# The beginning of a two-layer step: token norm from token rows, modulation pairs and projection units interleaved

## The reference, cut to what matters

```python
m = silu(cvec) @ w_ada[l] + b_ada[l]            # (6 * 1024); sh1, sc1, g1, sh2, sc2, g2
h = (x * rsqrt(mean(x * x) + 1e-6) * norm1_g[l]) * (1 + sc1) + sh1
p = h @ w_in[l]                                 # (1024, 2816): q_A, k_A, v_A, u_B, q_C, k_C, v_C
```

## Time and profile before

| | before |
|---|---|
| three runs, us | 1532.72, 1535.53, 1537.12 |
| profiled execution, span from first to last instruction, us | 1532.4 |
| TensorE busy, share of the span | 97% |
| VectorE busy | 61% |
| ScalarE busy | 51% |
| mean granted TensorE clock | 0.991 |
| DMA, mean over the span | 223 GB/s |

### The profile page before, as it was taken

The page is one execution under the profiler, slowest core; times in us unless marked ns, Lnnn a source line. Parts: engine busy times, 40 slices in busy tenths (PEclk is TensorE's granted clock), DMA queues, the critical chain, the costliest instruction groups (busy, mean ns, idle before and its releaser), DMA issues.

```text
span 1532.4 us, 22129 instructions
## 1 busy us (share of the span) xinstructions
PE 1484.4 (97%) x8652; PEld 1306.1 (85%) x8652; DVE 937.5 (61%) x1076; ACT 786.3 (51%) x892; POOL 53.6 (4%) x54
## 2 busy tenths in 40 slices
PE   5999999999999999999999999998999999999997
PEld 4788969689999999998889697898888888888875
DVE  3542265455654354436523665556898898988988
ACT  5434354353532242225333454535778778787875
POOL 0100000000000000001000000000000000000002
PEclk8999999999999999999999999999999999999999
DMA  9754375583763445245333554535899999999994
GB/s 332 242 178 155 110 226 187 178 262 110 231 195 111 125 115 160 84 150 170 121 117 110 180 186 158 193 114 176 313 375 387 379 376 371 380 386 374 377 378 164
DMA packets 236028, 342.36 MB, mean 223 GB/s; under 512 B 8629, under 2 KB 156766, under 8 KB 235694
## 3 DMA queue, kind: packets, MB, share of 16 engines
q1 hardware_dynamic: 227392, 313.32, 60.0%
q0 software_dynamic: 6496, 24.69, 4.4%
q10 hardware_dynamic: 2062, 3.24, 0.6%
HBM read 325.74 MB, written 15.47 MB: 223 GB/s over the span
## 4 chain that ended last, share of the span: by engine, by line
PE 87%; DVE 5%; DMA 3%; ACT 2%; SPq 1%; issue 1%; DVEq 0%; ACTq 0%
PE ps L648 25%; PE ps L650 25%; PE ps L649 25%; PE ps L665 2%; DMA raw<-in_w_ada_dram 2%; DVE wlo L2075 2%; PE ps L831 1%; SPq L446 1%; ACT whi L1508 1%; PE ps L865 1%; PE ps L849 1%; DMA early<-in_w_ada_dram 1%; PE ps L1063 1%; PE ps L731 1%; PE ps L810 0%
## 5 line engine op out<-in xcount | busy, mean ns | idle before, releaser
L648 PE MATMUL ps<-hhi,whi 128*128 128x384 f32 x824 | 276.7, 336 | 0.2
L650 PE MATMUL ps<-hhi,wlo 128*128 128x384 f32 x824 | 275.4, 334 | 0.0
L649 PE MATMUL ps<-hlo,whi 128*128 128x384 f32 x824 | 275.3, 334 | 0.0
L1696 DVE TENSOR_TENSOR wlo<-raw,whi 128x2048 fp32r<-128x2048 f32 x66 | 151.0, 2289 | 179.2 <-ACT whi L1258 165.9
L2075 DVE TENSOR_TENSOR wlo<-raw,whi 128x2048 fp32r<-128x2048 f32 (+1 forms) x81 | 179.0, 2227 | 27.4 <-ACT whi L1508 26.9
L1508 ACT ACTIVATE whi<-raw 128x2048 fp32r<-128x2048 f32 (+1 forms) x81 | 150.5, 1868 | 49.4 <-PE ps L650 49.2
L2075 DVE TENSOR_TENSOR wlo<-mraw,whi 128x2048 fp32r<-128x2048 f32 (+2 forms) x81 | 160.7, 1992 | 16.7 <-ACT whi L1508 16.2
L648 PE MATMUL ps<-whi,xgh 128*128 128x512 f32 (+1 forms) x432 | 163.9, 379 | 4.9 <-DVE wlo L2075 3.7
L1508 ACT ACTIVATE whi<-mraw 128x2048 fp32r<-128x2048 f32 (+2 forms) x81 | 136.6, 1687 | 51.4 <-PE ps L650 51.2
L650 PE MATMUL ps<-whi,xgl 128*128 128x512 f32 (+1 forms) x432 | 161.0, 373 | 0.0
L649 PE MATMUL ps<-wlo,xgh 128*128 128x512 f32 (+1 forms) x432 | 160.8, 372 | 0.0
(11 more groups left out here) (343 smaller groups left out, 2496.1 us busy)
## 6 DMA issues: line engine op xcount, KB each, us to landing
raw<-in_w_ada_dram SPq DMA_DIRECT2D x82, 512.0 KB, 5.6
raw<-in_w_ex_up_dram SPq DMA_DIRECT2D x27, 1024.0 KB, 6.4
raw<-in_w_ex_down_dram SPq DMA_DIRECT2D x27, 1024.0 KB, 5.0
raw<-in_w_gate_dram SPq DMA_DIRECT2D x48, 512.0 KB, 4.7
raw<-in_w_in_dram SPq DMA_DIRECT2D x44, 512.0 KB, 5.7
raw<-in_w_ex_gate_dram SPq DMA_DIRECT2D x18, 1024.0 KB, 7.1
mraw<-in_w_ex_gate_dram SPq DMA_DIRECT2D x18, 1024.0 KB, 7.8
mraw<-in_w_ex_down_dram SPq DMA_DIRECT2D x18, 1024.0 KB, 8.5
```

The lines of the kernel that those rows point to most:

```text
L648: pe.matmul(out, s[0], m[0], start=first, stop=False, **kw)
L649: pe.matmul(out, s[0], m[1], start=False, stop=False, **kw)
L650: return pe.matmul(out, s[1], m[0], start=False, stop=last, **kw)
L1696: dve.tensor_tensor(wlo[:, n % RING, :], raw[:, n % RING, :], whi[:, n % RING, :].bitcast(F32), ALU.subtract).then_inc(lo_done, 1)
```

## The change

Order of loads: only the identity part of the constants (64 KB) comes first, the rest after the modulation slots; the tokens come in three transfers with a semaphore each. Slots are renumbered (`FIRST_ADA`, `FIRST_WIN`): modulation 0 and 1, projection slot 0, modulation 2 and 3, projection slot 2 (the first half of K_A), modulation 4 to 7, projection slots 1 and 3. `win_turn` maps the k-th projection slot in this order. The small loads needed first go first, and lambda and sink have their own semaphore.

Norm: ScalarE squares the token rows as loaded and sums along them in the same instruction (`token_squares`), instead of squares of `xT`, VectorE sums and thin matmuls. VectorE, not ScalarE, copies the turned tokens to `xT`. TensorE spreads the root (`spread`) before modulation pair 0.

Projection: `first_units` does Q_A and the first slot of K_A pair by pair, with the modulation products between. 20 matmuls on the identity, into a bank that is overwritten later, stand before it.

```diff
+FIRST_ADA = (0, 1, 2, 3, 4, 5, 7, 9)
+FIRST_WIN = {0: 6, 2: 8, 1: 10, 3: 12}
+EARLY_BUF = {0: 0, 1: 1, 2: 2, 3: 3, 4: 4, 5: 0, 7: 1, 9: 2}
 # SyncE
+            sp.dma_start(ident, const[:, 0:P]).then_inc(const_in, 16)
+            for b in range(BLK):
+                sp.dma_start(xtok[:, b, :], a["x_sample"][0, (b - 1) * P:b * P] if b else a["x_prompt"][0]).then_inc(x_in[b], 16)
+            modulation(0, range(0, 2))
             projection_slot(0, 0)
+            modulation(0, range(2, 4))
+            projection_slot(0, 2)
+            modulation(0, range(4, 8))
+            sp.dma_start(cst[:, P:C_POOL], const[:, P:C_POOL]).then_inc(const_in, 16)
             projection_slot(0, 1)
...
 # TensorE
+            def first_units(products):
+                def pair(u, p, b):
+                    return products(u, b, (2 * p, 2 * p + 1))
+                pe.wait_ge(x_ev, BLK)
+                pe.wait_ge(lo_done, split_count(win_slot(0, 0) + 1))
+                pe.wait_ge(h_ready, 1)
+                for b in range(BLK):
+                    if b == 2:
+                        ada_pair(1)
+                    pair(Q_A, 0, b)
+                ada_end(0, 1)
+                pe.wait_ge(lo_done, split_count(win_slot(0, 2) + 1))
+                for b in range(BLK):
+                    if b == 2:
+                        ada_pair(2)
+                    pair(K_A, 0, b)
+                ada_end(0, 2)
+                pe.wait_ge(h_ready, 2)
+                for b in range(BLK):
+                    mm = pair(Q_A, 1, b)
+                mm.then_inc(mm_done, 1)
+                pe.wait_ge(ada_read, 3)
+                for b in range(BLK):
+                    if b == 2:
+                        ada_product(0, 6)
+                    mm = pair(K_A, 1, b)
+                mm.then_inc(mm_done, 1)
+                ada_product(0, 7)
+                ada_end(0, 3)
+                pe.wait_ge(lo_done, split_count(win_slot(0, 1) + 1))
+                for p in (2, 3):
+                    pe.wait_ge(h_ready, p + 1)
+                    for b in range(BLK):
+                        mm = pair(Q_A, p, b)
...
+                ada_product(1, 0)
...
             pe.wait_ge(const_in, 16)
             for b in range(BLK):
+                pe.wait_ge(x_in[b], 16)
                 for k in range(KD):
                     mm = pe.transpose(...)
                 mm.then_inc(x_tr, 1)
+                if b == 0:
+                    pe.wait_ge(init_in, 16 * n_init)
...
+            pe.wait_ge(v_ev, 2)
+            spread(0)
             pe.wait_ge(silc_ready, 1)
             pe.wait_ge(pick_ready, 1)
             ada_pair(0)
             ada_end(0, 0)
             pe.wait_ge(x_ev, BLK)
-            ada_pair(1)
-            ada_end(0, 1)
-            pe.wait_ge(ones_set, 1)
-            mean_squares(0)
-            ada_pair(2)
-            ada_end(0, 2)
+            for n in range(20):
+                pe.matmul(ps[:, 5, 0:P], ident, ident, start=True, stop=True)
 # ScalarE
             def ada_group(g):
+                act.wait_ge(mm_done, ada_slot(0, 2 * g + 1) + 1)
+                act.activation(adarow[:, :], ps[:, 7, 0:256], copy).then_inc(ada_row, 1)
+                if g == 0:
+                    hi(win_turn(0, 0))
                 act.wait_ge(ada_turned, g + 1)
...
+            def token_squares(b):
+                act.wait_ge(x_in[b], 16)
+                act.activation(xsq[:, b, :], xtok[:, b, :], ACT.Square, accum_out=rcol[:, 1, b:b + 1]).then_inc(sq_done, 1)
...
 # ScalarE, modulate(0): before pair p of the channel tiles
                         if p == 1:
+                            hi(win_turn(0, 1))
                         if p == 3:
+                            hi(win_turn(0, 2))
                             act.activation(lamp[:, :, :], lamp[:, :, :], ACT.Exp).then_inc(v_ev, 1)
+                        if p:
+                            ada_group(p)
 # VectorE
             def first_norm():
                 reciprocal_root(0)
+                for p in range(4):
                     scaled(0, p)
+                link(dve.tensor_tensor(lamprod[:, :, :], lamrow[:, :, 0, :], lamrow[:, :, 1, :], ALU.mult))
+                dve.tensor_reduce(lamp[:, :, :].rearrange("p l i -> p (l i)"), lamprod[:, :, :], X, ALU.add).then_inc(lam_sums, 1)
+                for p in range(4):
+                    first_modulations(p)
                     dve.wait_ge(mods_ready, p + 1)
                     shifted(0, p)
+                    if p < 3:
+                        lo(win_turn(0, p))
+                    h_low(0, p)
```

More of the change, by code:

```diff
@@ L700, in mean_squares @@
                     residual_turned(0)
[L701 to L705, removed]
+                spread(i)
                 if i in (1, 2):
@@ L732, in rot_transposes @@
                 mm.then_inc(tr_done, 1)
+            def first_units(products):
[30 more added lines that the diff above has]
+                    pe.wait_ge(h_ready, p + 1)
+                    for b in range(BLK):
+                        mm = pair(Q_A, p, b)
+                        if p == 3 and b < 2:
+                            mm.then_inc(proj_block, 1)
+                mm.then_inc(mm_done, 1)
+                ada_product(1, 0)
             def input_projection(l):
@@ L753, in input_projection @@
                         pe.matmul(proj_out(Q_A)[:, b, :], hlo[:, 0, b * P:(b + 1) * P], w[0], start=False, stop=False)
-                for p in range(4):
+                for p in range(4 if l else 0):
                     pe.wait_ge(h_ready, 8 * l + p + 1)
@@ L758, in input_projection @@
                     for b in range(BLK):
-                        if l == 0 and p == 1 and b == 2:
-                            ada_pair(3)
-                        mm = products(Q_A, b, (2 * p, 2 * p + 1) if p or l == 0 else (1,))
+                        mm = products(Q_A, b, (2 * p, 2 * p + 1) if p else (1,))
                         if p == 3 and b < 2:
@@ L779, in input_projection @@
                                 mm.then_inc(proj_block, 1)
-                            if i == 0 and b and u <= V_A:
+                            if i == (l == 0 and u == K_A) and b and u <= V_A:
                                 ti = 2 * (u - 1) + b - 1
@@ L1590, in _ @@
                            ACT.Silu).then_inc(silc_ready, 1)
-            for b in range(BLK):
-                act.wait_ge(x_tr, b + 1)
-                act.activation(xT[:, :, b * P:(b + 1) * P],
-                               ps[:, 2 * b:2 * b + 2, :].rearrange("p a (k t) -> p (a k) t", t=P), copy).then_inc(x_ev, 1)
-            act.wait_ge(x_ev, BLK)
-            for m0, m1 in ((0, 2), (2, 4), (4, 6), (6, 7), (7, 8)):
-                square(m0, m1)
-            ada_group(0)
-            act.wait_ge(ones_set, 1)
-            table(ACT.Sqrt)
-            ada_group(1)
-            hi(win_slot(0, 0))
-            root(0)
+            token_squares(1)
+            token_squares(2)
+            table(ACT.Sqrt)
+            root(0)
+            ada_group(0)
             act.wait_ge(lam_sums, 1)
@@ L1615, in _ @@
                             turned_evac(l, ti)
-                    if l == 0 and len(slots) == 2:
-                        hi(win_slot(l, slots[0] + 2))
+                    if l == 0 and len(slots) == 2 and u != K_A:
+                        hi(win_turn(l, slots[0] + 2 + (u == Q_A)))
                     if l == 0 and u == U_B:
@@ L1624, in _ @@
                     if l == 0:
-                        hi(win_slot(l, slots[-1] + 2))
+                        hi(win_turn(l, slots[-1] + 2 + (u == Q_A)))
                 pool_copy(l)
@@ L2210, in _ @@
                 for u, slots in enumerate(PROJ_SLOTS):
-                    if l or len(slots) == 2:
-                        lo(win_slot(l, slots[0] + 2))
+                    if l or (len(slots) == 2 and u != K_A):
+                        lo(win_turn(l, slots[0] + 2 + (l == 0 and u == Q_A)))
                     if l and len(slots) == 2:
                         lo(win_slot(l, slots[1] + 2))
+                    if l == u == 0:
+                        dve.wait_ge(const_in, 32)
                     if u < N_ROT:
@@ L2217, in _ @@
                     if l == 0:
-                        lo(win_slot(l, slots[-1] + 2))
+                        lo(win_turn(l, slots[-1] + 2 + (u == Q_A)))
                 for o in range(3):
```

116 lines of the change are left out of this document (50 added, 66 removed).

## The result

| | before | changed |
|---|---|---|
| runs, us (median; lowest to highest) | 1534.46 (1532.72 to 1537.12), 4 runs | 1545.67 (1541.93 to 1546.68), 4 runs |
| ratio to before, 95% interval | | 1.0065, 1.0051 to 1.0079 |
| profiled execution, span, us | 1532.4 | 1539.8 (its run: 1541.93, the lowest of the four) |

The change costs 0.65%, about 10 us, where 0.6 us of gain was forecast. (A ratio here is not the quotient of the two medians: those are 11.2 us apart.) The first part of the page of the changed kernel, to be read against the earlier trace rows: 22 matmuls and 22 weight loads more.

What follows compares the result with a forecast made beforehand. TensorE's late first projection product (34.83 us, behind the sixth modulation slot) and the low clock were taken to bound the beginning. 2.5 us gained minus 1.9 for one low spell gave 0.6: 1534.9 us, range 1530.0 to 1538.5.

Steps and rivals of the forecast that it cites:

- The ledger of the beginning: Step-by-step times from inputs to the mark: 64.6 against 67.05, 2.5 us gained if the clock stays up.
- Spread done: Norm on ScalarE, then TensorE's spread at the low clock level, 1.65 us, finished at 15.8 us; before, 29.2.
- pair 1: First modulation pair, queued behind the spread: 32 matmuls at the low clock level, 3.9 us, done at 19.7.
- first product: TensorE's first product of the input projection, forecast at 26.6 us, 8.2 us earlier than 34.83.
- gap: TensorE idle 3.6 us before K_A, waiting for VectorE's low half behind the second modulation; K_A starts at 36.6.
- one low spell: One low-clock stretch, after the dummies or behind the gap, taken as 1.9 us lost; chance 0.42.
- the mark: 67.05 us before: Q_A, K_A's first half, two transpose groups and the next modulation phase's first product done; forecast 64.6.
- The rival with the clock as the bound: Dummies don't lift the clock and it is low again after the gap: 3.1 us lost, 1538.6; chance 0.18.
- The price of the dummies: 20 dummy matmuls before the projection, 4.3 us at 0.216 each, from 21.2 to 25.5, said to cost nothing.
- The step that failed: Behind the mark both kernels have the same work and order, so the change is worth the mark's shift, 2.5 us.
- but for the transposes: Exception to same work behind the mark: one group of transposes before it, the other group counted as 0.6 us.
- The prediction's own sign of this: Stretches behind the mark differing by more than a microsecond would show the change acts somewhere not counted.

Runs made afterwards that it cites:

- 9 dummies: Changed kernel with 9 identity matmuls of 128 columns in place of 20; 1539.71 us, ratio 1.0033.
- 9 wide: Changed kernel with 9 dummy matmuls of 288 columns in place of 20 of 128; 1537.02 us, ratio 1.0014.
- 9 wide with both mends: Changed kernel with 9 dummies of 288 columns, K_A's low half before the second modulation, Q_A's transposes together behind K_A's second slot's block 1; 1529.31 us, ratio 0.9964.
- 9 thin with both: 9 wide with both mends, but its 9 dummies have one column each; median 1531.72 us, ratio 0.9981.
- before with 11: Kernel before plus 11 dummy matmuls where TensorE waits 2.69 us for the first row copy; 1541.57 us, ratio 1.0043.
- transposes together: Changed kernel with both groups of Q_A's transposes behind block 1 of K_A's second slot; 1542.35 us, one run.
- low half first: Changed kernel with VectorE's low half of K_A's first slot ahead of the second modulation; 1537.50 us, one run.
- 31 dummies: Changed kernel with 31 dummy matmuls in place of 20; 1539.03 us, ratio 1.0025.
- 31 with both mends: Changed kernel with 31 dummies, K_A's low half first and both transposes behind block 1 of K_A's second slot; 1533.18 us, ratio 0.999.
- before with 22: Kernel before plus 22 dummy matmuls at the same place as in before with 11; 1538.02 us, ratio 1.0018.

## Why the prediction was wrong

All kernels, sorted by the matmul and load records that TensorE has over the 2 x 8652 of the kernel before, all of them ahead of the loop. The last column says how the distance to the kernel before changes between 500 and 562 us, over the turn of the loop (the same matmuls laid beside each other; positive is lost):

| added | kernels | the branch, us | idle at the pass's first matmul | stall at its 15th | pieces fetched in the second pass | over the turn, us |
|---|---|---|---|---|---|---|
| 0 | before, 9 dummies, 9 wide, 9 wide with both mends, 9 thin with both | 4.0 to 4.4 | 1.2 to 1.6 | none | 9 | -0.3 to 0.1 |
| 44 | changed (twice), before with 11, transposes together, low half first | 3.3 to 3.9 | 0.5 to 1.1 | 2.1 to 2.9 | 9 | 3.0 to 4.1 |
| 88 | 31 dummies, 31 with both mends, before with 22 | 0.23 to 0.24 | none | none | 0 | -1.8 |

Point by point:

- **The ledger of the beginning** held. Spread done at 14.9 (forecast 15.8), pair 1 at 18.3 (19.7), first product 24.96 (26.6), gap 3.57 (3.6) with VectorE's low half ending it, K_A 35.30 (36.6), one low spell of 3.4 us right behind the gap and none at the first products, 1.1 us won at the mark (0.6). The landings and the order on VectorE were read well enough. The rival with the clock as the bound had the right side, a loss, by luck: of its two low spells only the one behind the gap is there, the beginning was a gain all the same, and the loss came from elsewhere and is larger than its 3.1 us. The price of the dummies was luck too: 20 transposes at the low level, 0.216 us each, where they are 40 records at the high level, 0.12 each. And the spread ran at the high level (0.91 us, forecast 1.65), while the low spell came behind it, from 15.0 to 18.4.
- **The step that failed** stands in "What bounds the kernel now": "From the mark on both kernels have the same work in the same order, but for the transposes, so the change is worth what it moves the mark by." Same work and same order are not the same program. TensorE's stream got 44 instructions longer ahead of the dense loop. That costs 0.43%, 6.6 us, by two pairs of kernels: 11 dummies in the kernel before (1.0043), and nine wide dummies for twenty narrow ones in the changed one (1.0057 to 1.0014; by the ends of the two intervals 0.13% to 0.74%). I priced the dummies by their time, 4.3 us beside VectorE's chain; that time was near (4.71 us, and nothing waited for them) and beside the point. The prediction's own sign of this came out: "if the stretches behind the mark differ by more than a microsecond, the change acts somewhere that I didn't count".
- **A smaller miss in the same sentence**: "but for the transposes". The second group stands right ahead of Q_C and adds a wait of 1.0 us to the 0.6 that it costs as work anywhere, and that eats what the mark had won. Together with the gap it was worth mending: from nine wide dummies to the same with both mends, 1.0014 to 0.9964, 0.5%.
- **The sum, as measured** in the later runs: 0.57% = 0.43% for the place of the instructions + 0.14% that are left with nine wide dummies, which the gap, its low spell and the transposes more than cover.

What the 6.6 us consist of is shown in part only. In the changed kernel's profile 2.4 us of stall and 1.7 us of the low spell behind it lie at 554 to 561, less 1.0 us for the shorter idle time at the pass's beginning: 3.2 us net over the turn of the loop, 3.1 in the kernel before with 11 dummies. The next ones (a low spell of 6.8 us at 697 where the kernel before has 3.4, one at 1059, a wait of 2.6 us at L658 for `xgl` where it was 1.2) come and go between kernels and profiled executions; that they follow from the stall through the times at which transfers meet is argued, not shown. The wait for `xgl` is 2.4 to 2.8 us in all kernels with 44 added and in one of three with 88, and 1.2 or less in all others. A second open point is the wait for a modulation slot near 290: one piece of 2.0 us or more in the kernels with 44 and 88, pieces of at most 1.9 without. A third: why with 44 added a piece is waited for at the 15th matmul of the pass, where without them the corresponding piece comes in time and the wait is at the branch alone. I could see the fetches, not where in the code each block begins, so the place of the boundary is inferred from where TensorE stops (the same matmul in all five profiles) and when the fetch starts.

The Trainium skill, "Runtime: NRT & Kernel Launch", section "Instruction fetch mechanics", says that streams are refilled in 16 KiB blocks of 256 instructions (the traces agree on the size: 16 KB a piece), that crossing a boundary is mostly hidden (they agree for nearly all), and that a taken branch whose target isn't in the window held forces a fetch before execution goes on. This last rule bore on the change, and I hadn't weighed it. The traces agree with it at the branch: 3.3 to 4.4 us where the pass is fetched again, 0.23 us where nothing is. They add a second place, some 6 us behind it (the branch is at 548.3 in the trace, TensorE stops at 554.7), and only for one of three positions.

## What to carry to other kernels

An instruction added to an engine's stream has two prices, its time and its place: whatever follows in a loop is shifted against the blocks in which instructions are fetched. Where TensorE is 97% busy, look in the trace for a matmul that waits for "issue" inside a group whose operands are all there, with an instruction transfer just starting; if it is new, pad or thin out the stream ahead of the loop (here nine wide dummies for twenty narrow ones) before judging the edit. Look at the loop's branch too: the backward branch that took 3.3 to 4.4 us instead of 0.23 was the one behind which the pass was fetched again, and the profile put part of the wait down to VectorE. And before a reorder is dropped as slower, test it at another position of the same code. Here the position alone brought 1.0057 to 1.0014; with the two mends of the beginning the same reorder is 0.36% faster than the kernel before. The version with nine wide dummies, both mends and 88 instructions more, which would also save the idle time at the branch (1.8 us as an estimate from the last column), was not run.

## What was unexpected of the hardware

- The turn of a loop of some 1626 matmul and load records costs TensorE 1.2 to 1.6 us, or 2.6 to 4.0 us in two pieces, or nothing, by the number of instructions ahead of the loop (0, 44, 88). With 88 the second pass fetches no instructions at all. Everything else in the kernel can stay as it was.
- An idle time of 2.2 us ahead of the first product, behind 4.61 us of wide dummies, was followed by a low spell (0.50 in 26.1 to 29.5); 0.95 us behind 4.71 us was not, nor 1.05 us behind the same 4.61. Nor was the idle time of 2.69 us of the earlier trace rows, so the length of the idle time alone doesn't decide.
- ScalarE started right on behind its table load in the changed kernel too (load 11.82 to 13.10, next activation 13.11), and a square with sum has a second instruction of 0.19 us behind it:

```profile
9.63 1.04 ACT L1646 ACTIVATE xsq<-xtok 128x1024 f32<-128x1024 f32 x1
10.57 0.19 ACT L1646 ACTIVATION_READ_ACCUMULATOR xsq<-xtok 128x1 f32 x1
...
11.82 1.28 ACT L1301 ACT_TABLE_LOAD   x1
13.11 0.20 ACT L1301 ACTIVATE fin<-epsc 128x1 f32<-128x1 f32 x1
```
